# A norm of its own for each of two token streams at four block borders of a three-pass fp32 transformer kernel

## What is computed

```python
def sandwich_ffn(x, w_gate_up, w_down, g_pre, g_post, shift, scale, gate):
    h = modulate(rms_norm(x, g_pre), shift, scale)
    return x + 0.5 * gate * rms_norm(swiglu(h, w_gate_up, w_down), g_post)
...
    x = x + mx[5] * rms_norm(out_x, g[3])       # out_x, out_c = token_mix(hx, hc, ...)
```

## Time and profile before

| what | value |
|---|---|
| runs | 3254.95, 3267.02, 3269.36 us, median 3267.02 |
| profiled execution | span 3252.7 us |
| TensorE busy | 3041.1 us (93%) |
| VectorE busy | 1679.5 us (52%) |
| ScalarE busy | 1353.6 us (42%) |
| first stack | from 0 to about 1850 us |

### The profile page before, as it was taken

One profiled execution on the slowest core, in us unless ns is written; L12 is line 12 of the kernel. 1 busy time (PEld: TensorE's weight loads), 2 busy tenths in 40 slices (PEclk: granted clock), 3 DMA queues, 4 the chain that ended last, 5 costly groups with the idle time before them and its releaser, 6 DMA issues. The chain is left out here.

```text
span 3252.7 us, 52824 instructions
## 1 busy us (share of the span) xinstructions
PE 3041.1 (93%) x21680; PEld 2676.5 (82%) x21680; DVE 1679.5 (52%) x2538; ACT 1353.6 (42%) x2092; POOL 230.6 (7%) x318
## 2 busy tenths in 40 slices
PE   6999989989999899997889899998999999989998
PEld 4777858657777688876789889998799889988998
DVE  3222264553222633235655557656675687556765
ACT  3222242532222432233455455546464555454644
POOL 1111015101110000011300000000000000000000
PEclk9999989989999899998989999999899999999999
DMA  8555244135554232344245543644265446543553
GB/s 290 164 172 181 91 145 126 40 130 164 172 181 134 87 104 90 108 152 125 67 155 188 169 149 117 195 156 138 67 206 187 160 147 198 193 142 117 167 183 104
DMA packets 406475, 476.80 MB, mean 147 GB/s; under 512 B 11084, under 2 KB 383388, under 8 KB 406282
## 3 DMA queue, kind: packets, MB, share of 16 engines
q1 hardware_dynamic: 380176, 389.05, 37.2%
q0 software_dynamic: 25248, 84.71, 8.5%
q10 hardware_dynamic: 858, 0.29, 0.0%
HBM read 470.71 MB, written 4.84 MB: 146 GB/s over the span
## 5 line engine op out<-in xcount | busy, mean ns | idle before, releaser
L422 DVE TENSOR_TENSOR w_lo<-w_raw,w_hi 128x1024 fp32r<-128x1024 f32 x734 | 897.5, 1229 | 1245.3 <-ACT w_hi L419 1244.2
L430 PE MATMUL bank<-a_hi,w_hi 128*128 128x256 f32 (+1 forms) x3864 | 1243.1, 322 | 57.7 <-DVE a_lo L1434 16.4
L431 PE MATMUL bank<-a_lo,w_hi 128*128 128x256 f32 (+1 forms) x3864 | 1228.3, 318 | 0.0
L432 PE MATMUL bank<-a_hi,w_lo 128*128 128x256 f32 (+1 forms) x3864 | 1227.4, 318 | 0.0
L419 ACT ACTIVATE w_hi<-w_raw 128x1024 fp32r<-128x1024 f32 x734 | 770.5, 1056 | 969.1 <-PE bank L432 950.0
L430 PEld LDWEIGHTS bank<-a_hi,w_hi 128*128 128x128 f32 x3864 | 743.1, 192 | 133.2 <-issue 76.3
L432 PEld LDWEIGHTS bank<-a_hi,w_lo 128*128 128x128 f32 x3864 | 743.2, 192 | 50.4
L431 PEld LDWEIGHTS bank<-a_lo,w_hi 128*128 128x128 f32 x3864 | 744.0, 193 | 47.9
L430 PE MATMUL bank<-h_hi,w_hi 128*128 128x256 f32 (+1 forms) x1728 | 544.4, 315 | 0.0
L432 PE MATMUL bank<-h_hi,w_lo 128*128 128x256 f32 (+1 forms) x1728 | 539.5, 312 | 0.0
L431 PE MATMUL bank<-h_lo,w_hi 128*128 128x256 f32 (+1 forms) x1728 | 539.4, 312 | 0.0
(11 more groups left out here) (289 smaller groups left out, 2286.4 us busy)
## 6 DMA issues: line engine op xcount, KB each, us to landing
w_raw<-in_mlp_w SPq DMA_DIRECT2D x128, 1024.0 KB, 5.3
w_raw<-in_w_ffn_gate_up SPq DMA_DIRECT2D x88, 1024.0 KB, 5.2
m_raw<-in_w_mod POOLq DMA_DIRECT2D x128, 512.0 KB, 4.8
w_raw<-in_w_ffn_down SPq DMA_DIRECT2D x32, 1024.0 KB, 5.9
w_raw<-in_gla_w_in SPq DMA_DIRECT2D x24, 1024.0 KB, 5.3
w_raw<-in_w_in SPq DMA_DIRECT2D x16, 1024.0 KB, 5.9
w_raw<-in_ple_w_gate SPq DMA_DIRECT2D x16, 1024.0 KB, 5.2
w_raw<-in_w_ffn_down SPq DMA_DIRECT2D x16, 768.0 KB, 5.7
```

What stands on the lines that cost most here:

```text
L422: e.tensor_tensor(w_l, raw, w_h.bitcast(F32), ALU.subtract).then_inc(S.lo_ready.sem, 1)
L430: e.matmul(dst, hi, rhs_hi, start=start, stop=False)
L431: e.matmul(dst, hi, rhs_lo, start=False, stop=False)
L432: return e.matmul(dst, lo, rhs_hi, start=False, stop=stop)
```

## The change

At the four borders with two streams, `crossing` takes the place of the last two slots of the old block (`tail`, `tail + 1`), of `post_norm` and `pre_norm`, and of the first two slots of the next block (`h`, `h + 1`). Every one of these slots is gone through twice, first with x's 256 columns and then with the context's (in the last layer's mixing block the queries need x alone). Each stream has its own sums, root, reciprocal, spread and factors. The order on every engine is written out by hand. The feed-forward parts are cut at 14 and 8 hidden tiles, the modulation rows skip the first pair and the last slots, the loads of the attention bias move up behind the second tail slot, and `TT_SHIFT` becomes 80. Cut to its core:

```diff
-TT_SHIFT, T_SHIFT = 0, (80, 80, 80, 80, 80)
+TT_SHIFT, T_SHIFT = 80, (80, 80, 80, 80, 80)
...
-            def ffn(layer, f, n, mod_a, mod_down, mod_b, mod_down_b=0):
-                pre_norm(layer, 4 * f, 6 * f, n, layer == 0 and f == 0)
-                parts = [(0, 16), (16, FT - 16)] if n == TT else [(0, FT)]
...
+                gate_up(w_gu, 0, 0 if at.crossed is None else 1, FT_A // 2, TT, mod_a)
...
+                crossing(w_d[FT_A * P:, :], rhs, S.dve_evicted, (layer, 4 * f + 1, 6 * f + 2, 0.5), head)
...
+            def stream_products(n, s, b, rhs, used, ready=None, steps=None):
+                c, steps = slice(s * T, s * T + T), steps or {}
+                order = [(k, m) for k in range(DK) for m in range(2)] if ready else [(k, m) for m in range(2) for k in range(DK)]
+                for k, m in order:
...
+                        if ready and m == 0:
+                            e.wait_ge(ready[k][0].sem, ready[k][1])
...
+                    if (m, k) in steps:
+                        steps[m, k]()
...
+            def crossing(w_tail, rhs, by, post, head):
+                gemm(w_tail, [(0, DK)], 2, 2, rhs, to_z(TT, add), by, sums=z_sums(TT, by, True), goes_on=True)
...
+                stream_products(tail, 0, 0, rhs, S.x_done)
+                stream_products(tail + 1, 0, 2, rhs, S.x_done, **joint_pending)
...
+                def begin_x():
+                    keep(1, 4, (S.slot_used, a_used + 1))
+                    ahead(tail, None, 0, (0,))
+                    X.spread_root()
+                    for k in range(3):
+                        X.scale(k)
+                    X.add_pair(0)
+                    X.square_pair(0)
+                stream_products(tail, 1, 0, rhs, S.slot_used, steps={(0, 0): first_sums, (0, 4): last_of_x, (1, 3): begin_x})
...
+                stream_products(tail + 1, 1, 2, rhs, S.slot_used, steps={(0, 4): sums_a, (0, 7): on_half, (1, 2): sums_b, (1, 6): sums_c})
+                keep(1, 7, (S.slot_used, a_used + 4))
...
+                X.sum_pair(3)
+                X.root_of()
+                C.square_tail(7, by, out_of[1, 7])
+                ahead(tail + 1, None, 0, (1,), lo=False)
+                ahead(tail, None, 0, (1,), hi=False)
+                X.invert()
+                X.spread_root()
...
+                X.prepare_all({4: C.invert})
+                ahead(tail + 1, None, 0, hi=False)
...
+                stream_products(h, 0, 0, a_rhs, used, ready=X.done, steps={(1, 1): C.spread_root})
+                head.keep(0, 0, (used, first))
...
+                stream_products(h + 1, 0, 2, a_rhs, used, steps={(1, 3): sums_d, (1, 7): sums_e})
...
+                C.sum_pair(2)
+                C.sum_pair(3)
+                C.root_of()
+                head.keep(0, 1, (used, first + 2))
+                if not head.both:
+                    ahead(h, None, 0)
+                C.invert()
+                C.spread_root()
+                C.prepare_all()
+                if head.both:
+                    stream_products(h, 1, 0, a_rhs, S.slot_used, ready=C.done)
+                    ahead(h, None, 0)
+                    head.keep(1, 0, (S.slot_used, h_used))
+                    stream_products(h + 1, 1, 2, a_rhs, S.slot_used)
+                    ahead(h + 1, None, 0)
+                    head.keep(1, 1, (S.slot_used, h_used + 2))
...
+            class FeedForward:
+                def keep(self, s, j, used):
...
+                            e.activation(tmp_g[:, m, c], bank[m][:, c], ACT.Silu).then_inc(S.act_evicted.sem, 1)
...
+                            e.tensor_tensor(tmp_y[:, m, c], tmp_g[:, m, c], bank[2 + m][:, c], ALU.mult).then_inc(S.dve_evicted.sem, 1)
...
+                    if j == 0 and s == 0:
+                        fetch_table(ACT.Sqrt)
```

More of the change, by code:

```diff
@@ L75, in __init__ @@
         self.a, self.d, self.h, self.l, self.v, self.slot = a, d, h, l, v, slot
+class Renorm:
+    def __init__(self):
+        self.factors, self.rooted, self.inverted, self.spread, self.scratch_free = 0, 0, 0, 0, 0
+        self.squared, self.tail, self.scaled, self.added, self.squared_pair, self.summed, self.high, self.done = ({} for _ in range(8))
 class Place:
@@ L617, in gemm @@
                 rep(pairs // per, body, peel=ready is not None, loads=mod_per > 0)
-                if sums:
+                if sums and not goes_on:
                     sums(pairs - 1)
@@ L688, in body @@
                         cut_hidden(i, p, per, n, (base.d, base.h))
[L689 to L692, removed]
+                if first_p > p0:
+                    body(None, p0, 1, 0)
+                times = (pairs - first_p) // per
+                rep(times, lambda i, start: body(i, first_p + start * per, per, mod_per), peel=base.slot == 0,
+                    loads=mod_per > 0)
+                if (pairs - first_p) % per:
+                    body(None, pairs - 1, 1, 0)
+                at.slot += (pairs - p0) * each
                 at.lag = (0, 2)
                 for s in (S.act_evicted, S.dve_evicted, S.hidden_hi, S.hidden_lo):
[L695 removed]
+                    s.n += 2 * (pairs - p0)
                 if mod_per:
[L697 removed]
+                    mods_done(2 * per * times, times)
             def to_z(n, add=False):
@@ L990, in hidden_ready, with ffn @@
                 at.a_ready = {tiles - 2: (S.hidden_lo, n - 1), tiles - 1: (S.hidden_lo, n)}
-            def ffn(layer, f, n, mod_a, mod_down, mod_b, mod_down_b=0):
-                pre_norm(layer, 4 * f, 6 * f, n, layer == 0 and f == 0)
-                parts = [(0, 16), (16, FT - 16)] if n == TT else [(0, FT)]
+            def ffn(layer, f, mod_a, mod_down, mod_b, head):
                 w_gu, w_d = A["w_ffn_gate_up"][layer, f], A["w_ffn_down"][layer, f]
[L997 to L1008, removed]
@@ new lines, in walk, with __init__, when_read, source @@
+            class Queries:
+                def __init__(self, layer, last):
+                    self.w, self.pre, self.both, self.layer = A["w_in"][layer], (layer, 2, 3), not last, layer
+                    self.out = []
+                def when_read(self):
+                    bias_loads(self.layer)
+                def source(self, j):
+                    return matrix(self.w)[:, :, j * SC:j * SC + SC]
+                def keep(self, s, j, used):
+                    c = slice(s * T, s * T + T)
+                    for m in range(2):
+                        if act:
+                            e.wait_ge(used[0].sem, used[1] + m + 1)
+                            e.activation(qk[:, 2 * j + m, c], bank[2 * j + m][:, c], ACT.Copy, scale=HEAD_DIM ** -0.5).then_inc(S.act_evicted.sem, 1)
+                    S.act_evicted.n += 2
+                    self.out.append(S.act_evicted.n)
+                def free(self, j):
+                    if pe:
+                        e.wait_ge(S.act_evicted.sem, self.out[j])
+                def end(self):
+                    at.lag = (2, 0)
@@ L1338, in pool_products, with bias_loads @@
                 return products
-            def mix(layer, last):
-                n = T if last else TT
-                pre_norm(layer, 2, 3, TT)
+            def bias_loads(layer):
                 if pool:
                     side_wait()
[L1345 to L1348, removed]
+                    e.wait_ge(S.slot_used.sem, 2 * (at.slot - 2))
                 for qt in range(2):
@@ L2456, in network @@
                 yield
[L2457 to L2464, removed]
+                yield ffn(0, 0, 1, 2, 1, Queries(0, False))
+                yield mix(0, False, FeedForward(0, 1))
+                yield ffn(0, 1, 1, 2, 1, FeedForward(1, 0))
+                yield ffn(1, 0, 0, 0, 1, Queries(1, True))
+                yield mix(1, True, None)
+                yield ffn_last(1, 1)
                 for i in range(DEPTH_2):
```

333 lines of the change are left out of this document (319 added, 14 removed).

## The result

The changed kernel takes 3281.28 us (median of 5 runs, 3270.40 to 3282.92), the one before 3254.95 us on the same chip (5 runs, 3252.09 to 3269.36). The ratio is 1.0064 with a 95% interval of 1.0042 to 1.0086: slower by 0.6%, where 3237 us and faster were forecast. The 3267.0 us on which the forecast stood was the median of three runs and 12 us high; taken as a ratio, the forecast was 0.991.

What follows compares the result with a forecast made beforehand. TensorE, busy 93% of the span, was taken as the bound, its idle time lying mostly at four borders. Gains of 21.6 (borders), 5.1 (start) and 3.2 (shift) made 29.9 us off 3267.0: 3237 us, range 3203 to 3262.

Steps and rivals of the forecast that it cites:

- The step that failed: Outside the borders: the shift saves 0.0067 us on each unshifted 256-column product, 3.2 us at most.
- R2: Rival: the shift also speeds up 512-column products by 0.0067 us each, 35 us, giving 3202 us; chance 0.12.
- (a) to (g): Terms of the border stretch: context tail, two gaps, head passes and eviction wait; borders together gain 21.6 us.
- the wait on `tmp_y`: Term (g), at two borders: `gate_up` waits for the last evictions of the head, 3.0 us.
- R1: Rival: at each border, waits move instead of going, another 4 us; 3253 us, no change; chance 0.22.
- Start: Program start: a first pair without modulation rows lets products begin near 44 us and gains 5.1 us.
- 14/8 split: Feed-forward parts: the split has the same number of slots and products, so no term in the sum.
- R3: Rival: the clock holds through both short gaps at the borders, about 18 us less, 3219 us; chance 0.08.
- R4: Rival: half-size head passes stay at 1.2 GHz, about 60 us more in all, 3297 us, slower; chance 0.08.
- The table load: ScalarE at the borders: priced by the row at 1.283 us, against about 2.7 us from the skill.

Runs made afterwards that it cites:

- b_shift80: The kernel before with `TT_SHIFT` 80 instead of 0 and nothing else: 3288.41 us, ratio 1.0113.
- b_pad160: The kernel before with an unused tile of 640 bytes behind `stat`, displacing the block regions: 3273.0 us, ratio 1.0055.
- a_end_shift0: The changed kernel with `TT_SHIFT` 0 and the two new tiles behind the block regions, so nothing is displaced: 3252.15 us, ratio 0.9989.
- a_nocross: `a_end_shift0` with `post_norm` and `pre_norm` in place of the crossings and bias loads moved back; 14/8 split and modulation order stay: 3262.41 us, ratio 1.0020.
- a_best: `a_end_shift0` with evictions ahead of slot h + 3's low cuts and, at the last border, slot h + 2's cuts moved: 3243.38 us, ratio 0.9962.

## Why the prediction was wrong

**The step that failed** is "The shift gives 0.0067 us for each 256-column product that was unshifted ... 3.2 us at most". It read 0.120 and 0.1133 us from unshifted and shifted slots, rightly, and took the shift to do nothing to products of 512 columns, of which there are more than ten times as many. No row of before has such a product shifted, so its cost had no bound from the trace; R2 bounded it on the side of a gain only (35 us). The measured effect has R2's size, almost, and the other sign: 31.4 us lost in `b_shift80`, which has all 5,328 products of 512 columns; the changed kernel has 4,656 of them left. There, beside the displacement, the shift costs 10.2 us. Two levels of pace in rows 4 had shown that the address of the weights sets the step; that was reason to put an equal amount on both sides.

**Left out altogether** were the two new tiles. The prediction counted instructions and not bytes of memory, and said that the forecast is wrong "if the attention, whose code is not touched, moves". The second stack moved, by 16 us in the profiled execution. Some 6.5 of these are the slower products with `h` that `b_pad160` also shows; the rest is no effect of these tiles: the largest part, 7.6, is the lower clock in one attention section, which other executions with this layout don't show.

Together, up to the mark: `a_end_shift0` is at 1641.9, 5.4 us ahead of before. The displacement alone adds 7.3 (the changed kernel's 1,296 products of 512 columns with `h` at 0.0056 more are 7.3). The shift on top adds 10.2: 3,360 products with `a` at 0.006 are 20.5, of which products with `h` give back 1,296 x 0.0038 = 4.9 and those of 256 columns some 5 to 7. That makes 12.1. By the ratios of the runs the same three parts are -0.11%, +0.42% and +0.33% of the whole kernel, 20.8 us; the profiled execution of the kernel after, the longest of its five, shows 28.5.

The other steps:
- **(a) to (g), the border.** Right in kind and in place: at its first border the kernel after has a tail that ends at 27.1 us (27.1 forecast), gaps of 5.4 and 5.9 (4.7 each), 14.6 and 13.1 for the head passes, and later 3.44 and 3.55 for the wait on `tmp_y` (3.0). Its first stretch is 66.2 (64.1). The tail's figure is partly luck: its products step by 0.1171 and not 0.1133, 0.7 us in all, and the bursts of sums cost as much less. The gains are mis-sized: 9.7 us in all without the address effects, of 21.6 forecast. At the feed-forward heads, where 4.2 were forecast, 0.1 and 0.6 are left, because six small terms were all taken too short, and the fall of the clock behind the wait on `tmp_y`, 1.6 us at each, was in no term. R1 forecast just such lengthenings, 4 us at each border; they were 1.5 to 4.1, mean 3, and nearly 4 with the clock's part. Of the rivals R1 is the one that tells the borders rightly.
- **Start.** The first product came at 43.57 (forecast near 44). But the first slot, partly cold, took 13.9 us, where some 11.2 were forecast. In `a_end_shift0`, without the address effects, it took 13.0 and the second ended at 67.5, where it had ended at 72.0 before. Less 2.2 for the modulation rows still owed that is 2.3 us of the 5.1.
- **14/8 split.** Taken as free. `a_nocross` reaches the mark at 1651.8 where before has 1647.3; with the 2.3 us of the start, 6.8 us are lost. By the times at which the blocks begin and end, about 4 us go in the first of the three feed-forward blocks with two streams and about 3 in the third; the second is level. Why was not found out.
- **R2** has the wrong sign. **R3** is refuted: the clock fell in both short gaps, to 0.51 from 461.20 to 465.80 and 0.53 from 481.80 to 486.50. **R4** as well: it was 1.00 for the rest of either pair of passes, 0.1133 us a step from 466.00. The kernel became slower by a way that none of the rivals named: "slower" had 0.08, all of it for R4.
- **The Trainium skill** (TensorE: Matmul & The Clock Gate, "Wait — 56ns, not 53.3ns?") gives 215.7 ns for a warm matmul of 512 columns. No product here reaches it: they take 227 to 234 ns, and the distance of the operands moves them over 7 of these. The measurement decides.
- **The table load** was set against the Trainium skill (ScalarE: Activation LUTs, "What ACT_TABLE_LOAD costs") as two different prices. The section's total of about 2.7 us is a load of about 1283 ns and a drain behind it. The load agrees with the row's 1.283 us; a drain is not seen here, since in the kernel before ScalarE's next instruction starts 11 or 12 ns behind 32 of the 33 loads. The sum was right to go by the row.

## What to carry to other kernels

Where TensorE is the bound, a change of addresses is a change of its own: compare the step of an untouched product in both traces before reading any wait, and test shift and layout alone. New tiles go behind the large operands, or their size is tried as an unused tile first. A gain that is the difference of many small waits, each forecast at its shortest, came out at less than half here (9.7 us of 21.6). And a total from one trace is split into sections and held against the median of the runs before it is explained: of the 16.4 us behind the mark here, about half were the kernel's and half that one execution's.

## What the runs showed of the hardware

- A warm fp32r matmul of 512 columns steps by 0.2271, 0.2290, 0.2328, 0.2333 or 0.2342 us by the distance between weights and moving operand: up to 3%, or 31 us of this kernel (`b_shift80`). At 256 columns the steps are 0.1133 to 0.1153, 0.1178 and 0.120, and the best distance is another. Which property of the addresses decides stays open; the three products of high and low parts were not taken apart.
- An unused tile of 160, 320 or 640 bytes made the second stack's 3,048 products with `h` step by 0.1200, 0.1199 and 0.1178 us in place of 0.1153 to 0.1167, with no instruction changed.
- Two faults of layout can hide each other: 320 bytes of shift and 640 of displacement give `h` 0.2290, less than either alone (0.2333, 0.2328).
- Within one execution and one layout, whole sections of 256-column products with `a` run at 0.1133 or at 0.1178 us a step. The cause is open.
- A wait of 3.46 us on an eviction (`a_end_shift0`, 1129.01) was followed by a clock of 0.86 over 12 us, one of 0.9 us (`a_best`, 1125.31) by 1.00.
